# Running sums of decays: eight groups of TensorE broadcast products against one set of rows, stored to DRAM and broadcast by GpSimd's DMA queue

## The reference, cut to what matters

```python
def ssd_chunked_scan(x, dt, a, bmat, cmat):
    xd = (x * dt[..., None]).reshape(b, nc, L, G, HG, SSM_HEAD_DIM)
    a_cs = jnp.cumsum((dt * a).reshape(b, nc, L, G, HG), axis=2)
    ...
    a_t = jnp.moveaxis(a_cs, 2, -1)
    decay = jnp.exp(jnp.where(causal, a_t[..., :, None] - a_t[..., None, :], -jnp.inf))
    cb = jnp.einsum('bclgn,bcsgn->bcgls', cc, bc)
    y_diag = jnp.einsum('bcghls,bcsghp->bclghp', cb[:, :, :, None] * decay, xd)
    decay_to_end = jnp.exp(a_cs[:, :, -1:] - a_cs)
    states = jnp.einsum('bclgn,bclghp->bcghpn', bc, xd * decay_to_end[..., None])
    ...
    y_off = jnp.einsum('bclgn,bcghpn->bclghp', cc, prev) * jnp.exp(a_cs)[..., None]
    return (y_diag + y_off).reshape(b, s, N_SSM_HEADS, SSM_HEAD_DIM)
```

## Time and profile before

| | |
|---|---|
| median of 3 runs | 1501.96 us (1501.89 to 1503.2) |
| span of the profiled execution | 1499.5 us, slowest and only core |
| PE busy | 1454.8 us, 97% of the span |
| DVE busy | 986.3 us, 66% |
| ACT busy | 742.6 us, 50% |
| POOL busy | 15.4 us, 1% |
| DMA | 501.79 MB, mean 335 GB/s |

### The profile page before, as it was taken

One profiled execution on the slowest core, in us unless ns is written; L12 is line 12 of the kernel. 1 busy time (PEld: TensorE's weight loads), 2 busy tenths in 40 slices (PEclk: granted clock), 3 DMA queues, 4 the chain that ended last, 5 costly groups with the idle time before them and its releaser, 6 DMA issues.

```text
span 1499.5 us, 18721 instructions
## 1 busy us (share of the span) xinstructions
PE 1454.8 (97%) x6964; PEld 986.3 (66%) x6964; DVE 986.3 (66%) x1258; ACT 742.6 (50%) x977; POOL 15.4 (1%) x18
## 2 busy tenths in 40 slices
PE   7989999999999999999999999999999989999998
PEld 2836787888789888675567456765465655565573
DVE  2578788888569889776466446765654565655662
ACT  3575544443456885354446245644453453545460
POOL 0000000000000000002000000000000000000000
PEclk9999999999999999999999999999999999999999
DMA  9878698888376335677999999999999999999995
GB/s 361 329 261 290 244 395 307 294 297 294 92 228 170 99 110 207 260 290 304 401 420 420 408 417 415 419 419 421 410 420 414 419 419 411 418 415 415 419 420 231
DMA packets 117019, 501.79 MB, mean 335 GB/s; under 512 B 13636, under 2 KB 16349, under 8 KB 81849
## 3 DMA queue, kind: packets, MB, share of 16 engines
q1 hardware_dynamic: 115640, 496.51, 85.2%
q0 software_dynamic: 1280, 4.01, 0.8%
HBM read 498.33 MB, written 2.29 MB: 334 GB/s over the span
## 4 chain that ended last, share of the span: by engine, by line
PE 86%; DVE 6%; DMA 5%; ACT 2%; issue 1%; SPq 0%; DVEq 0%; ACTq 0%
PE acc L2648 18%; PE acc L3144 17%; PE acc L2656 17%; PE acc L2649 17%; DMA raw<-in_moe_w_down 3%; DVE w_lo L1565 2%; PE xb L3034 1%; PE acc L2797 1%; DMA raw_rest<-in_moe_w_down 1%; PE xb L3075 1%; PE xb L2696 1%; DMA raw<-in_ada_w 1%; PE acc L3268 1%; PE acc L3263 1%; PE acc L3261 1%
## 5 line engine op out<-in xcount | busy, mean ns | idle before, releaser
L1565 DVE TENSOR_TENSOR w_lo<-raw,w_hi 128x1024 fp32r<-128x1024 f32 x354 | 424.9, 1220 | 188.3 <-ACT w_hi L1025 178.7
L1025 ACT ACTIVATE w_hi<-raw 128x1024 fp32r<-128x1024 f32 x354 | 369.2, 1057 | 283.1 <-PE acc L2656 155.3
L2648 PE MATMUL acc<-w_hi,g_hi 128*128 128x512 f32 x448 | 180.0, 402 | 3.9 <-ACT w_hi L1025 3.9
L2649 PE MATMUL acc<-w_hi,g_lo 128*128 128x512 f32 x448 | 175.0, 391 | 0.0
L2648 PE MATMUL acc<-w_hi,a_hi 128*128 128x512 f32 x384 | 153.6, 400 | 0.8
L2649 PE MATMUL acc<-w_hi,a_lo 128*128 128x512 f32 x384 | 149.9, 390 | 0.0
L2656 PE MATMUL acc<-w_lo,g_hi 128*128 128x512 f32 x448 | 138.7, 391 | 2.5 <-DVE w_lo L1565 2.5
L3144 PE MATMUL acc<-raw,g_s 128*64 128x512 f32 x544 | 120.5, 594 | 0.0
L2656 PE MATMUL acc<-w_lo,a_hi 128*128 128x512 f32 x384 | 118.4, 390 | 0.0
L2648 PEld LDWEIGHTS acc<-w_hi,g_hi 128*128 128x128 f32 x448 | 84.1, 188 | 42.6 <-issue 18.0
L1565 DVE TENSOR_TENSOR w_lo<-mod,w_hi 128x1024 fp32r<-128x1024 f32 x68 | 80.7, 1219 | 30.8 <-ACT w_hi L1025 28.7
(11 more groups left out here) (408 smaller groups left out, 2083.0 us busy)
## 6 DMA issues: line engine op xcount, KB each, us to landing
raw<-in_moe_w_gu SPq DMA_DIRECT2D x134, 1024.0 KB, 14.2
raw<-in_moe_w_down SPq DMA_DIRECT2D x66, 1024.0 KB, 17.6
raw<-in_ada_w SPq DMA_DIRECT2D x96, 512.0 KB, 6.0
mod<-in_moe_w_gu SPq DMA_DIRECT2D x42, 1024.0 KB, 13.9
raw<-in_ffn_w_gu SPq DMA_DIRECT2D x56, 512.0 KB, 5.6
raw_more<-in_moe_w_gu SPq DMA_DIRECT2D x23, 1024.0 KB, 14.4
mod<-in_moe_w_down SPq DMA_DIRECT2D x23, 1024.0 KB, 16.4
raw<-in_ssm_w_in SPq DMA_DIRECT2D x40, 512.0 KB, 4.7
```

What stands on the lines that cost most here:

```text
L1025: act.activation(w_hi[:, w % SPLIT, :], raw_tile(no), ACT.Copy).then_inc(hi_ready, 1)
L1565: dve.tensor_tensor(w_lo[:, w % SPLIT, :], raw_tile(no), r32(w_hi[:, w % SPLIT, :]), ALU.subtract).then_inc(raw_used, 1)
L2648: pe.matmul(o, l_hi[:, k, rows_], hi[:, col:col + HALF], start=new, stop=False)
L2649: pe.matmul(o, l_lo[:, k, rows_], hi[:, col:col + HALF], start=False, stop=False)
```

## The change

PE's sums step makes two more products, with `dt_a` and the triangle in the other order, which leave the running sums as 32 rows of 256 tokens. DVE copies them to `dt_rows`. POOL stores them to DRAM (`acs_scratch`) and, for each unit, loads the 8 rows of its heads (one run of 4 KB) to all 128 partitions of the unit's half of `dec`. The loads of unit 2 and later wait for the y products of two units before. ACT's Relus read `dec` and write it in place. The 128 matmuls of L3278, accumulator pair 2's use for them, and their order numbers are gone.

```diff
@@ -274,6 +274,7 @@
     acc = [nc.alloc_psum_tensor(f"acc{n}", [P, 2 * HALF], f32) for n in range(3)]
     xb = [nc.alloc_psum_tensor(f"xb{n}", [P, HALF], f32) for n in range(2)]
     rel_dram = nc.dram_tensor("rel_scratch", (HEADS, 3 * P), f32, kind="Internal").ap()
+    acs_dram = nc.dram_tensor("acs_scratch", (T, SH, P), f32, kind="Internal").ap()
     hm_dram = nc.dram_tensor("hm_scratch", (SEQ, D), f32, kind="Internal").ap()
     token_dram = [nc.dram_tensor(f"token_scratch{rnd}", ((EXPERTS + 2 * T) * P, 16), f32, kind="Internal").ap() for rnd in range(2)]
     Y_ROWS = STORED * P
@@ -324,6 +325,8 @@
     u_ready, cv_ready, cs_ready = (sem(n) for n in ("u_ready", "cv_ready", "cs_ready"))
     dtv_ready, dte_ready, dta_ready, acs_ready, acse_ready = (
         sem(n) for n in ("dtv_ready", "dte_ready", "dta_ready", "acs_ready", "acse_ready"))
+    acs_rows, st_acs = sem("acs_rows"), sem("st_acs")
+    ld_acs = [sem(f"ld_acs{n}") for n in range(2)]
     state_ready, e_ready, mt_ready, y_ready, yss_ready, yms_ready, yroot = (
         sem(n) for n in ("state_ready", "e_ready", "mt_ready", "y_ready", "yss_ready", "yms_ready",
                          "yroot"))
@@ -1460,18 +1461,14 @@
             def unit_decays(u):
 
                 c, g = SUNITS[u]
-                q, used = unit_pair("a", u)
-                act.wait_ge(acc_full, full_no("a", u))
                 if u == 0:
                     act.wait_ge(acs_ready, 1)
-                if u >= 2:
-                    act.wait_ge(acc_full, full_no("y", u - 2))
+                act.wait_ge(ld_acs[u % 2], 16 * (u // 2 + 1))
                 for i in range(HG):
                     cols = slice(i * P, (i + 1) * P)
-                    ins = act.activation(dec[:, u % 2, cols], acc[q][:, cols], ACT.Relu, scale=-1.0,
+                    ins = act.activation(dec[:, u % 2, cols], dec[:, u % 2, cols], ACT.Relu, scale=-1.0,
                                          bias=acs[:, c, HG * g + i:HG * g + i + 1])
-                ins.then_inc(acc_done[q], 1)
-                act.wait_ge(acc_done[q], used + 1)
+                own(ins)
                 if u == 0:
                     act.activation(end_e[:, :, :], end_e[:, :, :], ACT.Exp).then_inc(acse_ready, 1)
                 act.activation(dec[:, u % 2, :], dec[:, u % 2, :], ACT.Exp, scale=-1.0).then_inc(e_ready, 1)
@@ -2248,7 +2245,9 @@
 
                 c = proj_piece["sums"]
                 dve.wait_ge(xb_full, c + 1)
+                dve.tensor_copy(dt_rows[:, :], xb[c % 2][0:SH, 2 * T * SH:2 * T * SH + SEQ]).then_inc(acs_rows, 1)
                 own(dve.tensor_copy(acs[:, :, :], xb[c % 2][:, 0:2 * T * SH].rearrange("p (t m) -> p t m", t=2 * T)))
+                dve.wait_ge(acs_rows, 1)
                 dve.sem_inc(xb_done[c % 2], 1)
                 own(dve.tensor_tensor(end_e[:, :, :], acs[:, T:2 * T, :], acs[:, 0:T, :], ALU.subtract))
                 dve.sem_inc(acs_ready, 1)
@@ -2600,6 +2599,14 @@
             pool.wait_ge(gain_used, 2)
             pool.dma_start(gain_row[:, :], bass.AP(A["norm_gain"].tensor, A["norm_gain"][1, 1:2, :].offset, [[0, P], [1, D]])).then_inc(ld_gain_late, 16)
             pool.sem_inc(yd_free, 2)
+            pool.wait_ge(acs_rows, 1)
+            pool.dma_start(acs_dram.rearrange("c h n -> h c n"), dt_rows[:, :].rearrange("h (c n) -> h c n", c=T)).then_inc(st_acs, 16)
+            pool.wait_ge(st_acs, 16)
+            for u, (c, g) in enumerate(SUNITS):
+                if u >= 2:
+                    pool.wait_ge(acc_full, full_no(u - 2))
+                pool.dma_start(dec[:, u % 2, :], bass.AP(acs_dram.tensor, acs_dram.offset + (c * SH + HG * g) * P, [[0, P], [1, HG * P]])).then_inc(
+                    ld_acs[u % 2], 16)
             pool.wait_ge(hm_rest, 4 * T)
             pool.wait_ge(hm_rows, T)
             pool.dma_start(hm_dram[0:SEQ, :].rearrange("(t p) n -> p t n", p=P), hm[:, :, :]).then_inc(st_hm, 16)
@@ -3215,7 +3222,9 @@
                 pe.wait_ge(dta_ready, 1)
                 b = open_piece(proj_piece["sums"])
                 for n in range(2 * T):
-                    mm = pe.matmul(b[:, n * SH:(n + 1) * SH], tri if n < T else ones, dt_a[:, n % T, :], start=True, stop=True)
+                    pe.matmul(b[:, n * SH:(n + 1) * SH], tri if n < T else ones, dt_a[:, n % T, :], start=True, stop=True)
+                for c in range(T):
+                    mm = pe.matmul(b[0:SH, 2 * T * SH + c * P:2 * T * SH + (c + 1) * P], dt_a[:, c, :], tri, start=True, stop=True)
                 mm.then_inc(xb_full, 1)
 
             def mixer_steps(i):
@@ -3273,17 +3282,12 @@
 
                 c, g = SUNITS[u]
                 pe.wait_ge(cs_ready, 4)
-                o = open_pair(*unit_pair("a", u))
-                for i in range(HG):
-                    mm = pe.matmul(o[:, i * P:(i + 1) * P], dt_a[:, c, HG * g + i:HG * g + i + 1].to_broadcast([P, P]), tri,
-                                   start=True, stop=True)
-                mm.then_inc(acc_full, 1)
                 b = open_piece(proj_piece["cb", u])
                 pe.matmul(b[:, 0:P], b_t[:, g, c * P:(c + 1) * P], c_t[:, g, c * P:(c + 1) * P], start=True, stop=True).then_inc(xb_full, 1)
 
             def unit_out(u):
                 c, g = SUNITS[u]
-                o = open_pair(*unit_pair("y", u))
+                o = open_pair(*unit_pair(u))
                 pe.wait_ge(mt_ready, u + 1)
                 if c == 0:
...
```

More of the change, by code:

```diff
@@ L654, in build, with full_no @@
     NU = len(SUNITS)
-    full_order = [("a", 0), ("a", 1)] + [w for u in range(NU) for w in ([("y", u)] + ([("a", u + 2)] if u < NU - 2 else []))]
-    def full_no(what, u):
-        return len(UNITS) + full_order.index((what, u)) + 1
+    def full_no(u):
+        return len(UNITS) + u + 1
     PROJ_COLS = (2 * DI, 2 * DI + HALF) + tuple(DI + g * HALF for g in range(SG)) + tuple(g * HALF for g in range(SG))
@@ L673, in group_pair, with unit_pair @@
         return g % 2, base + g // 2
-    def unit_pair(what, u):
-        return (2, base + u) if what == "a" else (1, base + 3 + u)
+    def unit_pair(u):
+        return 1, base + 3 + u
     def opened_pair(stage, t):
@@ L682, in opened_pair @@
             return (pr0["wo"] + t) % 3, (pr0["wo"] + t) // 3
-        return ((2, base + NU), (0, base + 3 + SG))[t]
+        return ((2, base), (0, base + 3 + SG))[t]
     def y_piece(q, t):
@@ L732, in build @@
     moe_uses = [(FJ + 1) // 2, FJ // 2, 1]
-    pair_uses0 = [base + 3 + SG + 1, base + 3 + NU, base + NU + 1]
+    pair_uses0 = [base + 3 + SG + 1, base + 3 + NU, base + 1]
     ROUND0_HIGHS = len(G_BLOCKS) + EXPERTS // 2 * MIX_PIECES - len(G_BLOCKS)
@@ L949, in home_free @@
                 elif name == "more0":
-                    sp.wait_ge(acc_full, full_no("y", NU - 1))
+                    sp.wait_ge(acc_full, full_no(NU - 1))
                     sp.wait_ge(y_ready, NU)
@@ L1481, in state_out @@
             def state_out(u):
-                q, _ = unit_pair("y", u)
-                act.wait_ge(acc_full, full_no("y", u))
+                q, _ = unit_pair(u)
+                act.wait_ge(acc_full, full_no(u))
                 act.activation(state[:, :], acc[q][:, HALF:2 * HALF], ACT.Copy).then_inc(state_ready, 1)
@@ L2366, in unit_out @@
                 own(dve.tensor_tensor(y3, y3, heads_of(srow[:, 2, :], g).to_broadcast([P, HG, SHD]), ALU.mult))
-                dve.wait_ge(acc_full, full_no("y", u))
+                dve.wait_ge(acc_full, full_no(u))
                 if c == 0:
```

## The result

The changed kernel takes 1509.34 us (median of 8 runs, 1504.3 to 1513.24), the kernel before 1502.26 us: 7.1 us more by the medians, ratio 1.0039 with a 95% interval of 1.0027 to 1.0051 (the ratio is not the quotient of the two medians, which is 1.0047). Slower, by an interval that lies wholly above 1, and outside the forecast range of 1497.8 to 1507.5 us. The profiled execution took 1509.34 us with a span of 1507.5 us, so 1.8 us lie around a span.

A forecast was written before the change was run, and what follows sets the result against it. VectorE was taken to bound the scan: of 14.6 us of TensorE products removed, only 0.4 us would come out, mainly for the load's landing, so 1499.5 - 0.4 + 2.5 = 1501.6 us, range 1497.8 to 1507.5 us.

The forecast's parts named there:

- VectorE sets the pace, and passes on its three waits less 0.65 us, 3.0 us at most: In the scan, VectorE's three C·B waits of 3.7 us bound the gain, less 0.65 us for copy and Relus.
- Copy 0.42 us, Relus 2.4 us per unit: VectorE's added PSUM copy takes 0.42 us; ScalarE's Relus, reading SBUF, take 2.4 and not 2.18 us per unit.
- Landing 4.2 us: Each 512 KB load by POOL's queue takes 4.2 us from issue to landing, with bounds 3.0 and 12.2 us.
- The loop through units 5 and 7: Serial chain from unit u-2's y products to unit u's mask product, 11.7 us; unit 5 0.85 late, unit 7 0.45 early.
- the forecast -0.4: Net change in time at the scan's end: 0.45 us from unit 7's earlier mask product, taken as 0.4 us gained.
- TensorE's waits at L3290/L3293 ... of 1 to 4 us in most units: Expected trace sign: TensorE stands before the scan's y products for VectorE's release or mask product, 1 to 4 us.
- The sum: Whole forecast: 14.6 us of products go and 0.4 us come out; each us of load time counts twice.
- third rival: In the scan, loads land late, 6 to 8 us each, 3.6 to 7.6 us over forecast, 1505 to 1509 us; 24%.

The follow-up runs named there:

- e2: The changed kernel with loads into two buffers of their own, from which the Relus write dec: 1499.73 against 1502.56 us, ratio 0.998.
- e7: The changed kernel with loads into own buffers and 12 unread filling products before unit 1's y products: 1498.11 against 1503.32 us, ratio 0.9961.
- e11: The changed kernel with loads into own buffers, 12 unread filling products before and 8 behind unit 1's y products: 1500.12 against 1502.07 us, ratio 0.998.
- e3: The changed kernel with loads into own buffers and the eight broadcast products per unit kept as unread filling: 1503.1 against 1502.56 us, ratio 1.0005.
- e4: The kernel before with one broadcast product per unit instead of eight, nothing added: 2498.61 us with wrong decays; sums step to output projection 177.0 us.
- e8: The kernel before, products kept, plus the change's rows, copy, store and loads to buffers nobody reads: 1502.6 against 1503.32 us, ratio 0.9996.
- e6: The changed kernel with unread filling products before unit 1's y products and behind those of units 1, 3, 5: 1503.07 against 1503.32 us, ratio 0.9997.
- e10: The changed kernel with unread filling products only behind the y products of units 1, 3 and 5: 1505.86 us, ratio 1.0023.
- e9: The changed kernel with 12 unread filling products only before the y products of unit 1: 1508.5 against 1502.07 us, ratio 1.0038.
- e5: The changed kernel with each load from unit 2 on made twice, one after the other: 1521.08 against 1503.32 us, ratio 1.0111.

## Why the prediction was wrong

Its steps, with what the runs showed.

- *VectorE sets the pace, and passes on its three waits less 0.65 us, 3.0 us at most.* Right: S falls by 2.8 us where the load is out of the way (e2, e7, e11). 14.6 us of products are worth 4.0 us (e3 against e2), and 12.8 us of them 3.9 us with nothing added (e4), where the three waits held 3.7.
- *Copy 0.42 us, Relus 2.4 us per unit.* 0.41 us and 2.44 us; e8 has +0.6 us for all additions but the Relus' new source.
- *Landing 4.2 us.* 4.3 us (3.5 to 5.1 over the eight loads). The Trainium skill's fit ("DMA: Bandwidth & Descriptors", anatomy of one DMA on the GpSimd path) gave an estimate of 3.2 us, 1.1 us short. A slip that changed nothing: if each us counts twice, the 2.6 us from a gain of 0.4 to one of 3.0 are reached with a load of 4.2 - 2.6 / 2 = 2.9 us, not of 3.2 or 3.3.
- *The loop through units 5 and 7.* At a steady clock it held. The y products of unit 3 were forecast for 532.0 us, 0.6 us after those of before; e6, read on its own scale (its `dt_a` is 1.3 us earlier), has them at 532.4, the mask product of unit 5 at 543.29 + 1.33 = 544.6 (forecast 543.7), the y products of unit 5 at 552.4 (551.6) and the mask product of unit 7 at 563.10 + 1.33 = 564.4 (563.3):

```profile
543.29 1.23 DVE L2357 TENSOR_TENSOR dec<-dec,cbm 128x1024 f32<-128x1024 f32 x1 [0.65 <-ACT dec L1474]
...
551.06 1.12 PE L3303 MATMUL acc<-state,c_t 128*128 128x512 f32 x2 [0.60 <-DVEq L2376]
...
563.10 1.23 DVE L2357 TENSOR_TENSOR dec<-dec,cbm 128x1024 f32<-128x1024 f32 x1 [0.18 <-ACT dec L1474]
```

  They are 0.4 to 1.1 us late, and S is +0.7 us for the forecast -0.4. ScalarE waits for the load in units 4 to 7 of e6, by 2.6, 1.2, 2.2 and 0.2 us, about as the prediction named it. In the changed kernel itself, by the same reckoning (1.4 us there), the mask products of units 5 and 7 come at 545.7 and 568.3 us, 2.0 and 5.0 us late: the forecast path is there, and what the lower clock adds is not in it.
- *The step that failed: "TensorE's waits at L3290/L3293 ... of 1 to 4 us in most units", priced at nothing.* The prediction foresaw that TensorE would stand where it got shorter, and gave this idle time no price, since VectorE sets the pace. (It stood there for over 1 us in two units only, and twice in front of a z group instead.) But TensorE's clock fell at each idle time of 2.5 us and more, for 3.4 to 10.2 us, and this cost 6.4 us of S (188.0 against 181.6 us in e6). In the scan of before it never left its upper level, and e4 shows that the removed products kept it there: with them alone taken away, it falls. The Trainium skill ("TensorE: Matmul & The Clock Gate", Part 1) says that the clock gate follows how busy TensorE has been lately. The trace agrees, and a term for it was missing.
- *How it turns into time.* At the lower clock the y products of unit 1 take 2.3 us longer (5.0 and not 2.7 us from the first to the last) and a tile about 2.4 us longer (12 matmuls of 0.43 and not 0.23 us in the chain). In e2 neither reaches the end of S. In the changed kernel the y products start the next load, whose landing holds ScalarE, which holds the z copy, for which TensorE waits: a slow TensorE delays the loop. In the changed kernel that makes the 6.4 us. The size is measured; the path is read from the traces, and e2 and e10 support it: the same 10.2 us cost nothing without the loop and 2.9 us with it.
- *The even units.* The sum counted the landings of units 5 and 7 only and named the z copies behind ScalarE's wait in the third rival alone. ScalarE's two long waits for a load are those of units 4 and 6, and two of the three idle times came from them. In units 5 and 7 it did not wait for the load at all in the changed kernel. The third rival (slower, 24%) had the sign, but by a landing of 6 to 8 us, which did not happen; what it says of ScalarE holding the z copies is what the trace shows.

The changed kernel's eight runs spread over 9 us and e9's over 9.5, those of the other variants over 2 to 6. In these two, time and mean clock go together: from 1504.3 us at 0.993 to 1513.24 us at 0.984 of full speed in the changed kernel. So how much of the lower clock an execution gets varies, and the 6.4 us are the price in one execution each.

What stays open: why it varies. Single short falls of the clock among the experts, at about 1211 and 1430 us, differ from execution to execution. In the changed kernel's trace they come behind idle times of 1.6 and 2.1 us; in the kernel before 2.1 us at 1210 us passed without one. Nor was a loading of the rows by another queue tried.

## What to carry to other kernels

Work that is taken off an engine that is not the bound is worth only what the bound engine was losing to it; here 2.8 to 4.0 of 14.6 us, and it can be read beforehand from the waits of the bound engine. Taking it from TensorE has a second side: idle time of 2.4 us and more lowered its clock here, so a TensorE that was busy with work of little use may be slower without it, and a few products into an unused accumulator, put exactly in front of its waits, tell by one run whether that is the loss. A transfer that replaces a product belongs outside the loop between producer and buffer: a landing buffer of its own, freed by the first reader, made the same change about 9 us faster (ratio 0.998 and not 1.0039, S 178.1 and not 188.0 us).

## What the runs showed of the hardware

- In the scans of all traces TensorE's clock fell to 1.2 GHz at each of the 14 idle times of 2.44 us (e4) to 8.5 us (e5), for 3.4, 6.8 or 10.2 us, and at none of 0.6 to 1.84 us (the longest in e5). Among the experts falls came behind idle times of 1.6 and 2.1 us too (changed kernel), and one of 2.1 us passed without (kernel before).
- A load of 512 KB by GpSimd's queue, one 4 KB row to 128 partitions, landed in 4.2 to 4.9 us by the medians of the runs (e5 4.2, changed 4.3, e2 4.7, e8 4.9) with the DMA engines about half busy, and in 4.7 us where they were 80% busy (kernel before, 251 to 257 us; the earlier trace rows): the load on them hardly mattered. A store of 32 KB to DRAM by the same queue took 4.2 us in the changed kernel, as long as the 512 KB.
